# One PSUM bank per output group: the projection of a float32 transformer block as three 256-column products

## What is computed

```
proj = h @ w_in                       # h: 256 x 2048, w_in: 2048 x 11344
q_a, k_a, v_a, q_b, k_b, v_b, qi, ki, wi, g_a, g_b = split(proj)
y_a = stick_breaking_attention(q_a, k_a, v_a) @ w_a
y_b = dsa_attention(rope(q_b), rope(k_b), v_b, rope(qi), rope(ki), wi) @ w_b
merged = sigmoid(g_a) * y_a + sigmoid(g_b) * y_b
out = merged @ w_o
```

## Time and profile before

| what | value |
| --- | --- |
| time, three runs | 2655.48, 2656.82, 2658.40 us; median 2656.82 |
| profiled execution | time 2655.48 us, span of its instructions 2655.5 us |
| mean granted TensorE clock | 0.987 of 2.4 GHz |
| PE / PEld | 2599.2 us (98%) / 2242.1 us (84%) |
| DVE / ACT / POOL | 1880.6 us (71%) / 1232.6 us (46%) / 118.3 us (4%) |
| transfers | 560.52 MB, mean 211 GB/s |
| chain that ended last | PE 30%, DVE 1% of the span: PE L1843 20%, PE L1845 10% |

### The profile page before, as it was taken

How to read it: one execution, slowest core, us unless ns; L and a number is a source line. 1 busy time by engine, 2 the same in 40 slices (tenths; PEclk the granted TensorE clock), 3 DMA queues, 4 the chain that set the end, 5 groups by cost and what they waited for, 6 DMA issues and landing times. The chain is left out here.

```text
span 2655.5 us, 39667 instructions
## 1 busy us (share of the span) xinstructions
PE 2599.2 (98%) x14757; PEld 2242.1 (84%) x14757; DVE 1880.6 (71%) x2680; ACT 1232.6 (46%) x1607; POOL 118.3 (4%) x182
## 2 busy tenths in 40 slices
PE   6899999999999999999999999999999999999998
PEld 3588888888888888888888888887888888888887
DVE  2487778896888888855666658999776644566554
ACT  3345644444545555544555551115554444444443
POOL 0011122100010000000000000000000000000000
PEclk7899999999999999999999999999999999999999
DMA  9998689864786777755555544554666555666554
GB/s 375 347 300 260 218 253 279 260 211 157 238 269 208 258 247 253 232 191 188 190 190 189 187 163 143 151 151 130 195 183 190 190 188 188 188 189 190 187 186 135
DMA packets 523705, 560.52 MB, mean 211 GB/s; under 512 B 20408, under 2 KB 484537, under 8 KB 523321
## 3 DMA queue, kind: packets, MB, share of 16 engines
q1 hardware_dynamic: 503865, 488.51, 56.6%
q0 software_dynamic: 19712, 70.26, 8.6%
HBM read 553.45 MB, written 2.10 MB: 209 GB/s over the span
## 5 line engine op out<-in xcount | busy, mean ns | idle before, releaser
L1058 DVE TENSOR_TENSOR wlo<-raw,whi 128x1024 fp32r<-128x1024 f32 x794 | 969.8, 1224 | 596.6 <-ACT whi L638 589.7
L1843 PE MATMUL ps<-xhl,whi 128*128 128x512 f32 x4224 | 1333.6, 397 | 4.8 <-DVE wlo L1058 2.8
L638 ACT CAST whi<-raw 128x1024 fp32r<-128x1024 f32 x794 | 831.2, 1050 | 1031.4 <-PE ps L1845 993.1
L1845 PEld LDWEIGHTS ps<-xhl,wlo 128*128 128x128 f32 x4224 | 794.8, 188 | 187.2
L1845 PE MATMUL ps<-xhl,wlo 128*128 128x256 f32 x4224 | 831.6, 278 | 0.0
L1843 PEld LDWEIGHTS ps<-xhl,whi 128*128 128x128 f32 x4224 | 644.5, 189 | 8.8 <-issue 5.6
L1843 PE MATMUL ps<-ghl,whi 128*128 128x512 f32 x1024 | 319.6, 393 | 0.0
L1845 PEld LDWEIGHTS ps<-ghl,wlo 128*128 128x128 f32 x1024 | 192.3, 188 | 44.4
L2211 PE MATMUL ps<-xg,raw 128*128 128x256 f32 x1024 | 221.5, 379 | 0.0
L1843 PE MATMUL ps<-fhl,whi 128*128 128x512 f32 x704 | 219.4, 393 | 0.0
L2211 PEld LDWEIGHTS ps<-xg,raw 128*128 128x128 f32 x1024 | 194.7, 190 | 26.2
(11 more groups left out here) (316 smaller groups left out, 1564.6 us busy)
## 6 DMA issues: line engine op xcount, KB each, us to landing
raw<-in_w_in SPq DMA_DIRECT2D x176, 512.0 KB, 4.6
raw<-in_w_up SPq DMA_DIRECT2D x176, 512.0 KB, 3.5
ada<-in_w_ada POOLq DMA_DIRECT2D x128, 512.0 KB, 4.7
raw<-in_ffn_w_up SPq DMA_DIRECT2D x128, 512.0 KB, 3.6
raw<-in_ffn_w_down SPq DMA_DIRECT2D x128, 512.0 KB, 3.2
raw<-in_w_down SPq DMA_DIRECT2D x88, 512.0 KB, 3.2
att<-in_w_ada SPq DMA_DIRECT2D x32, 1024.0 KB, 11.2
raw<-in_conv_w_pw SPq DMA_DIRECT2D x128, 256.0 KB, 3.2
```

The source lines that it names most:

```text
L638: nc.scalar.copy(whi[t % SPL][:, :, :], raw[t % RAW][:, :, :]).then_inc(s_hi, 1)
L1058: nc.vector.tensor_tensor(wlo[t % SPL][:, :, :], raw[t % RAW][:, :, :], whi[t % SPL][:, :, :].bitcast(F32), ALU.subtract).then_inc(s_lo, 1)
L1843: mm(o[:, m, :, :], whi[t % SPL][:, c, m * P:(m + 1) * P], x, start=first and c == 0, stop=last and c == KC - 1, skip_group_check=True)
L1845: ins = mm(o[:, m, 0, :], wlo[t % SPL][:, c, m * P:(m + 1) * P], x[:, 0, :], start=False, stop=last and c == KC - 1, skip_group_check=True)
```

## The change

The diff below goes through the engines in the order ACT, DVE, PE. In the 42 groups and the small one, a pass of 512 columns of `whi` becomes two of 256, one against xh and one against xl, and both add into the same 256 elements as `wlo` against xh. So a half of a group needs 256 elements and the two halves one bank. Four banks form a ring, `one_bank(n)`, and PE waits before group G for group G-4 (for groups 2 and 3: for 0 and 1). ACT copies the bank to `att` in one instruction, at the step where it copied the xl part, and signals `s_free`. DVE has no sum in these groups; groups 0 and 1 stay as they were. The small group's copies by ACT are made straight from PSUM at step T_GATE. `low_nth` counts the `s_low` signals that are left.

```
-    return group + 1 - (group > G_WO + 7) - (16 if group >= G_PW1 else 0)
+    return group + 1 if group < 2 else group + 3 - G_WAB - (group > G_WO + 7) - (16 if group >= G_PW1 else 0)
...
+        def one_bank(n):
+            return ps[n % 2][:, n % 4 // 2, :, :]
...
+            def kept(G, t, first):
+                done(0, t)
+                nc.scalar.copy(att[:, first:first + PC, :], one_bank(G)).then_inc(s_free[G % 2], 1)
...
-                if s == T_SMALL // 2 + 2:
-                    act.wait_ge(s_kw, 1)
-                    nc.scalar.copy(kidx[0:64, :], part[G_SMALL % 2][0:64, 0, :]).then_inc(s_ki, 1)
-                    nc.scalar.copy(kidx[64:128, :], part[G_SMALL % 2][0:64, 0, :]).then_inc(s_ki, 1)
-                    nc.scalar.copy(wi_t[:, :], part[G_SMALL % 2][64:80, 0, :]).then_inc(s_free[G_SMALL % 2], 1)
...
-                if t <= T_SMALL and t % 4 == 0:
-                    low_out(0, t // 4 - 1, t)
+                if t == EARLY:
+                    low_out(0, 1, t)
+                if EARLY < t <= T_SMALL and t % 4 == 0:
+                    kept(t // 4 - 1, t, t // 2 - 2)
                 if t == T_GATE:
                     done(0, t)
-                    nc.scalar.copy(part[G_SMALL % 2][0:NSMALL, 0, :], ps[G_SMALL % 2][0:NSMALL, 0, 1, :]).then_inc(s_low, 1)
+                    keys = one_bank(G_SMALL)[:, 0, :]
+                    nc.scalar.copy(kidx[0:64, :], keys[0:64, :]).then_inc(s_ki, 1)
+                    nc.scalar.copy(kidx[64:128, :], keys[0:64, :]).then_inc(s_ki, 1)
+                    nc.scalar.copy(wi_t[:, :], keys[64:NSMALL, :]).then_inc(s_free[G_SMALL % 2], 1)
                 if t > T_GATE and (t - T_GATE) % 4 == 0:
-                    low_out(0, G_GATE + (t - T_GATE) // 4 - 1, t)
+                    n = (t - T_GATE) // 4 - 1
+                    kept(G_GATE + n, t, 8 + 2 * n if n < 8 else 48 + 2 * (n - 8))
...
-                if t <= T_SMALL and t % 4 == 0:
-                    kept(t // 4 - 1, t // 2 - 2)
-                if t == T_GATE:
-                    dve.wait_ge(s_low, low_nth(G_SMALL))
-                    few = part[G_SMALL % 2][0:NSMALL, 0, :]
-                    nc.vector.tensor_tensor(few, ps[G_SMALL % 2][0:NSMALL, 0, 0, :], few, ALU.add).then_inc(s_kw, 1)
-                if t > T_GATE and (t - T_GATE) % 4 == 0:
-                    n = (t - T_GATE) // 4 - 1
-                    kept(G_GATE + n, 8 + 2 * n if n < 8 else 48 + 2 * (n - 8))
+                if t == EARLY:
+                    kept(1, 2)
...
+            def one_bank_unit(t, G, rhs, first, last):
+                pe.wait_ge(s_lo, RAW + t + 1)
+                o = one_bank(G)
+                for c in range(KC):
+                    x = rhs(c)
+                    for w, half in ((whi, 0), (whi, 1), (wlo, 0)):
+                        for m in range(PC):
+                            ins = mm(o[:, m, :], w[t % SPL][:, c, m * P:(m + 1) * P], x[:, half, :],
+                                     start=first and c == 0 and w is whi and half == m == 0, stop=last and c == KC - 1, skip_group_check=True)
+                ins.then_inc(s_used, 1)
...
-                            pe.wait_ge(s_free[G % 2], G // 2 + 1)
+                            pe.wait_ge(s_free[G % 2], free_at(G - 4 if G >= 4 else G - 2))
                         rhs = from_x()
-                        unit(0, t, ps[G % 2], lambda c: rhs(4 * q + c), q == 0, q == 3)
+                        one_bank_unit(t, G, lambda c: rhs(4 * q + c), q == 0, q == 3)
```

More of the change, by code:

```diff
@@ L345, in build @@
         s_rd = sem("rotary_done")
-        s_kw = sem("index_key_and_head_weights_summed")
         s_ki = sem("index_key_copied")
@@ L2119, in _ @@
                         if t == T_SMALL:
-                            pe.wait_ge(s_free[G_SMALL % 2], G_SMALL // 2 + 1)
+                            pe.wait_ge(s_free[G_SMALL % 2], free_at(G_SMALL - 4))
                         pe.wait_ge(s_lo, RAW + t + 1)
                         wh, wl = (x[t % SPL][:, :, :].rearrange("p c n -> p (c n)") for x in (whi, wlo))
+                        o = one_bank(G_SMALL)[0:NSMALL, 0, :]
                         for c in range(DC // 2):
-                            w = slice(NSMALL * c, NSMALL * (c + 1))
                             k = DC // 2 * (t - T_SMALL) + c
-                            ins = products(ps[G_SMALL % 2][0:NSMALL, 0, :, :], wh[:, w], wl[:, w], xhl[:, k, :, :], k == 0, k == DC - 1)
+                            for w, half in ((wh, 0), (wh, 1), (wl, 0)):
+                                ins = mm(o, w[:, NSMALL * c:NSMALL * (c + 1)], xhl[:, k, half, :],
+                                         start=k == 0 and w is wh and half == 0, stop=k == DC - 1, skip_group_check=True)
                         ins.then_inc(s_used, 1)
```

## The result

The changed kernel takes 2663.94 us in the median (2662.95 to 2666.48), against 2656.05 for the kernel before on the same chip. The ratio is 1.0027, 95% interval 1.0018 to 1.0035: slower by 7 us, where 2654.4 and no measurable change had been forecast. The profiled execution has a span of 2661.2 us, 5.7 above that of before.

The account below looks back on a forecast made before the run. The prediction took PE's stream of matmuls, with few holes, to bound the changed stage. From 2655.5 us it added 0 for the products and -2.4 for holes: 2653.1, or 2654.4 on the median's scale, range 2642 to 2672.

Parts of the forecast that it names:

- The price of a short pass: PE products of the changed stage: six 256-column passes a chunk at 116 ns, 696 a cycle, no change (-4.7 to +3.4 us).
- first rival: PE products: overhead is paid per matmul, 14 ns each, so 18 us more, minus 2.4: 2670 us; chance 0.20.
- second form: PE weight loads: a load with its hand-over over 117 ns no longer fits under its pass; same slowdown, within the 0.20 chance.
- 0.349 a pair: Small group's 256 + 512 pair with 80-column loads: half of the 0.697 us cycle, so neither pass waits for its load.
- third rival: PE products: 3 ns fixed cost per matmul, 6 ns a cycle, +4 us, minus 2.4: 2658 us; chance 0.10.
- full PEld share: Weight loads in the changed stage: busy share goes to about 100%, which doesn't yet mean a bound.
- The holes: PE waits behind DVE additions in the changed stage: four times 0.6 us, 2.4 us gained, ends 0 and 6.
- the holes at 374 to 386 us: Three PE waits for wlo: bound by weight transfers, so they stay; 0.6 us at most gained, at 384.98.
- the ring of four: Banks in the changed stage: PE never waited for a bank, so the ring is worth nothing by itself.
- issue of 12 instructions a cycle: PE's queue, rival: one instruction in 58 ns may not hold; each ns above costs 8 us; chance 0.03.
- behind the stage: Kernel after 656 us: nothing may change there; if it does, the whole reading is incomplete.

Follow-up runs that it names:

- the products alone: Kernel before, with three 256-column passes in the 42 groups but two-bank tile, ACT copy, DVE sum and ring as before: 2668.51 us, ratio 1.0041.
- the read-out alone: Kernel before, same products, but no DVE sum in the 42 groups and ACT copying straight to att, whi by xl left out: 2652.56 us, ratio 0.9981.
- the moved sum: Kernel before, with DVE's sum of each of the 43 groups from group 1 on put one unit later in DVE's list: 2658.6 us, ratio 1.0001.

## Why the prediction was wrong

**The price of a short pass is the step that failed.** The prediction took 116 ns for a 256-column pass, from start steps of 115 and 117 in a mixed cycle, and half of the 233 of a 512-column pass. The runs show 120 in a run of its like. 4 ns x 6 x 672 is 16 us. With it the sum is 2656.8 + 16 - 2.4 = 2670, and 2666 with the 7.1 us of waits that went in place of 2.4; 2663.9 was measured. (The first rival gives 2670 as well, but its own terms, 18.1 us more and 2.4 less, make 2672.5.)

**Its first rival had the price right, and was held unlikely on the wrong row.** "The 57 ns of a cycle can be read as 14 ns for each of 4 matmuls" gave 724 ns; 720 was measured. What spoke against it, 233 and 115 where it wants 227 and 121, was a division by starts. With passes of equal length in a run, 227.5 and 119.9 is what they cost. In a mixture the long pass seems some 6 ns dearer and the short one some 5 ns cheaper. The total of a cycle comes out within 2 to 3 ns (697 against 695, 710 against 707.5), its parts don't. Why starts shift between passes of two lengths, no run shows.

**Its second form, a load that no longer quite fits, is not settled.** Against it: loads can follow each other every 112 ns also beside passes of 192 to 240 columns, as the prediction's row had it, and at 384 columns the width changes nothing. For it: at 256 columns, the length that counts here, a narrower load saves 2 to 6 ns of the 13, as much as the 4 ns by which the price was missed. So it is shown that a short pass costs 120 and that the products alone bring the loss; whether the last 4 ns are the matmul's or the load's part stays open.

**The small group was misread.** Its 0.349 a pair, half of the cycle, was taken to say that a shorter load doesn't shorten a pass. In the mixture it doesn't, and at 384 columns neither. But in a row of 256-column passes it does: 116 with the 80-column loads of the changed kernel's small group, where 128-column loads have 120. The 117 was near the price for its own loads; it couldn't be carried over to loads of 128.

**The third rival's size was wrong for these operands.** The fixed cost of 3 ns comes from plain float32 passes, 216 against 213. The passes of the split operands have 14 for the same time in the array. The rule of the Trainium skill, "TensorE: Matmul & The Clock Gate", section Back-to-back issue gap, has a fixed cost per matmul too, but its 2.5 ns are a fifth of what is measured here; by it the change would have cost 3.4 us in its passes and it cost 15. The same section gives the rule for a matmul by itself and says that in a stream of loads and matmuls both set the spacing, a condition that the prediction left out.

**The full PEld share was judged rightly.** PEld went to 99% of the stage while loads could still have followed faster: passes shortened from 256 to 240 columns with the same loads went from 120 to 112. Here the Trainium skill's "Perfetto Trace Analysis", section Identifying the Most-Contended Engine, would have pointed to the loads; the runs put the loss in the number of passes, each a matmul and its load, and a share of 99% doesn't say which of the two it was.

**The holes were undersized.** 0.6 us at each of four holes, 2.4 in all, against 5.1 measured for the read-out alone (2.6 to 7.4 by its interval; 4.0 in the stage) and 7.1 us of waits gone in the changed kernel. Each 0.6 was right, as the moved sum shows, but it was counted once for each hole. That DVE carries its lag from one group to the next, so that more than one sum stood before a hole, fits with it and with the waits that came up elsewhere when the sum was moved; no run measures it alone. And a slower PE hides waits by itself: 5.3 of 7.8 us in the run of the products alone. Of the changed kernel's 7.1 us no split between the two is given, as they overlap.

The prediction also wanted the holes at 374 to 386 us, which the transfers make, to stay. When only DVE is lighter they do, 2.8 us of them; in the changed kernel they are gone, and with the products alone 0.6 us is left.

**What held.** ACT's copy costs the same, PE waits for no bank in the traces of before and after (so the ring of four gave nothing that could be seen), issue of 12 instructions a cycle is sustained, and behind the stage little moved: from its end to the last instruction are 1999.2 us before and 2000.4 after.

## What to carry to other kernels

Price a matmul in a run of its like, with loads of the width that it will have: columns at the granted clock and a part that goes with each pass, checked against the totals of cycles with different numbers of matmuls. Start steps inside a mixture of lengths can carry a few ns from one length to the other, which is all it takes when thousands are added. Folding a sum into PSUM by cutting a 512-column pass in two saves an addition on another engine, but here cost 11 ns for each of 1344 added matmuls, 15 us, on the engine that sets the end, to free one that mostly had slack. Ask of any relief of a second engine how much of the first one's waits it can remove at most, and compare that with what the first one pays.

## What the runs showed of the hardware

A pass of the split operands (the type `fp32r` of `whi` and `wlo` in the profile) of 256 to 512 columns with its own load of 128 takes its columns at 2.4 GHz and 12 to 14 ns more (119.9 at 256, 173.6 at 384, 227.5 at 512), while a plain float32 pass of 256 columns takes 216, 3 more than the 213 of 512 columns. Where the extra comes from is open: at 384 columns not from the load's width (173 to 175 ns for 16 to 128 columns), at 256 columns in part from it (119.9 with 128, 113.9 with 64), and not from the bank or the order. Loads of 128 columns can follow each other every 112 ns beside passes of 128 to 240 columns. Between 240 and 256 columns the step climbs from 112.0 over 114.2 and 116.6 (248 and 252) to 119.9: 8 ns for 16 columns, which are 6.7 ns at 2.4 GHz. The records of loads fill PEld to 99% at a step of 120, where loads can follow every 112. A DVE operation with two operands in SBUF takes longer beside a POOL sum: 1477 ns where it takes 1220, and 1.6 to 1.9 us where it takes 0.68.
